# Recurrence input groups in a row, with the convolution read from the projection's PSUM banks

## The chip, the cores and the metric

One core of a Trainium2 chip runs one launch of a whole hybrid encoder layer. The metric is the device time in microseconds (us), the median over repeated runs. Names of engines: PE is TensorE, ACT is ScalarE, DVE is VectorE, POOL is GpSimd, SP is the queue that fetches the weights.

## What is computed

The layer has a residual stream of 512 tokens by 2048 channels. It is normalised and multiplied by one wide matrix w_in; the columns of the product are split among several consumers:

```
z = rms_norm(x, attn_norm) @ w_in
q_lat, kv_lat, k_rope_raw, g_mla, u_lru, g_lru, m_mla, m_lru = split(z)
xc = causal_dwconv(u_lru, conv_w, conv_b)          # 4 taps along the tokens, per channel
r = sigmoid(xc (block-wise) @ w_rg + b_rg)         # 16 blocks of 128 x 128
i = sigmoid(xc (block-wise) @ w_ig + b_ig)
log_a = -8 r softplus(-lam);  a = exp(log_a);  mult = sqrt(-expm1(2 log_a))
h = scan over tokens of  h[t] = a[t] h[t-1] + mult[t] i[t] xc[t]
y_lru = (h * silu(g_lru)) @ w_o_lru
y_mla = (attention(q_lat, kv_lat, k_rope_raw) * silu(g_mla)) @ w_o_mla
x = x + (sigmoid(m_mla) y_mla + sigmoid(m_lru) y_lru) @ w_out
```

A per-layer embedding with its own gate and a final norm follow. All is float32; products are kept accurate by splitting both operands into a high and a low part and adding three products.

## The kernel before

**Chunks.** The products with plain weights are made of chunks. A chunk is 128 rows of a weight matrix by 512 columns. For each chunk ACT writes its high part (whi, line 445, here called a split), POOL subtracts to get its low part (wlo, line 420), and PE runs 12 matmuls of 128 x 512 (lines 1544 and 1546 to 1554: four output tiles of 128 channels, three products each). The ring of split chunks holds four (RING), so the split of chunk k+4 waits until PE has finished chunk k (line 444). The ACT program is a list written by hand: a loop over the 16 chunks of a group, in each step ("slot k") the split for chunk k+4 and then whatever else has been placed at that k. Slot k can't begin before PE has finished chunk k of the current group.

**Groups.** A group is 16 chunks (K = 2048) that accumulate into four PSUM banks, one set of the two sets (0: banks 0 to 3, 1: banks 4 to 7). A set is claimed by PE when the semaphore released[set] has reached a number that is counted out (tables U_LRU, U_M2, U_LAT, lines 102 to 112). The stage that matters here runs these groups, in this order (lines 1681 to 1697): U0, U1, M2, U2, U3, Q, KV. U0 to U3 are the four groups of 512 channels of u_lru, M2 is the group of the last quarter of the merge gate m_mla, Q and KV are the latents. The last quarter of m_lru comes behind them, as the group M3.

**The recurrence of group i.** It needs these steps, on four tiles of 128 channels:

- DVE copies the four banks into upad, which has three zero columns in front (line 1206), releases the set, and makes the convolution of each tile from upad into xc with one tensor_scalar (line 1213) and three scalar_tensor_tensor (line 1216). After the second tile it makes gwlo (line 1220), the low part of the gate weights, and after each two tiles it makes xclo (line 999) from xc and ACT's xchi (line 598, lru_x).
- PE makes the gate products: gates(i, pair), line 1657, 12 matmuls for two tiles, in the middle of the group that follows: pair 0 behind its chunk 5+d, pair 1 behind its chunk 8+d (line 1678). They write into the set that group i itself had used.
- ACT makes the sigmoids r and i of a pair (lru_sigmoids, line 600, at slot 6+d and 8+d), the tanh (line 614), the exp (line 619, slot 9+d), the square (line 624, slot 10+d) and the square root (line 630, slot 11+d). Changes between these functions load another table on ACT.
- DVE multiplies ii by xc (line 1228), forms the argument of the root (line 1231), and then for each of four tiles does a multiply by the root (line 1236), the scan (line 1237) and the multiply by the output gate gg (line 1240). Only after these 12 operations does DVE go on to the next group.

In before the pairs use d = 0 for group 0 (inside U1), d = 4 for group 1 (inside M2), d = 0 for group 2 (inside U3) and d = 4 for group 3 (inside Q). Group U2 has no gate products in it.

**The merge gate.** When M2 is complete, ACT applies a sigmoid to its four banks into stage, and stores that (merge_gate_out, line 716, called at line 730, between two groups' loops, so behind slot 15 of M2 and ahead of slot 0 of U2).

**The latents.** DVE copies the four banks of Q (line 1247), computes the rotary angles, sums the squares, and so on; PE makes the sum of squares and the rotary keys' products behind chunk 12 of KV (line 1698).

Of the kernel before, what the change touches and what calls it, by code (L numbers as in the profile page):

```python
# [23 lines left out]
F32 = mybir.dt.float32  # L24
F32R = mybir.dt.float32r
# [38 lines left out]
def trunk_layer(nc, x, p, positions, vectors, conv_w, w_in, w_q_b, w_kv_b, w_rg, w_ig, w_o_mla, w_o_lru,  # L64
# [26 lines left out]
    C_M2 = C_LRU + 2 * KD  # L91
    C_LAT = C_M2 + 3 * KD
    C_U = (C_LRU, C_LRU + KD, C_M2 + KD, C_M2 + 2 * KD)
# [10 lines left out]
    U_LRU = (17, 18, 21, 21)  # L104
    SET_U = (1, 0, 0, 1)
    U_M2 = 20
# [24 lines left out]
    with ExitStack() as ctx:  # L131
# [14 lines left out]
        with ExitStack() as place:  # L146
# [36 lines left out]
        _, gg, upad, _, xc, xchi, xclo, rr, ii, _, graw, gwhi, gwlo = lay(  # L183
            ("lru_r1", [P, R1], F32), ("gg", [P, 4, S], F32),
            ("upad", [P, 4, S + 3], F32), ("upad_pad", [P, P - 16], F32), ("xc", [P, 4, S], F32), ("xchi", [P, 4, S], F32R),
            ("xclo", [P, 4, S], F32R), ("rr", [P, 4, S], F32), ("ii", [P, 4, S], F32),
            ("lru_pad", [P, R2 - 4 * S - P - 24 * S], F32),
            ("graw", [P, KD, 2 * P], F32), ("gwhi", [P, 4, 2 * P], F32R), ("gwlo", [P, 4, 2 * P], F32R))
        _, _, _, _, _, asq = lay(
            ("sq_r1", [P, R1], F32), ("sq_gg", [P, 4, S], F32), ("sq_upad", [P, 4, S + 3], F32),  # L190
            ("sq_pad", [P, P - 16], F32), ("sq_xc", [P, 4, S], F32), ("asq", [P, 4, S], F32))
# [125 lines left out]
        def _(sp):  # L317
# [46 lines left out]
            two_groups(C_M2, 0, ((w_in, m2), (w_in, COL_U + 2 * W)))  # L364
            two_groups(C_M2 + 2 * KD, 0, ((w_in, COL_U + 3 * W), (w_in, COL_Q)))
# [67 lines left out]
        def _(act):  # L433
# [176 lines left out]
            def lru_tanh(i, pair):  # L610
                if i == 0 and pair == 0:
                    act.wait_ge(sp_ready, 1)
                for t in (2 * pair, 2 * pair + 1):
                    act.activation(upad[:, t, 3:], rr[:, t], ACT.Tanh, scale=sp8[:, 4 * i + t:4 * i + t + 1]).then_inc(tanh_ready, 1)
# [11 lines left out]
            def lru_root(i):  # L626
                for t in range(4):

                    act.wait_ge(var_ready, 4 * i + t + 1)
                    act.activation(upad[:, t, 3:], upad[:, t, 3:], ACT.Sqrt).then_inc(mult_ready, 1)  # L630
# [14 lines left out]
            def lru_work(i, k, d):  # L645

                if k == 2 + d:
                    lru_x(i, 0)
                if k == 3 + d:
                    lru_x(i, 1)  # L650
                if k == 5 + d:
                    lru_x(i, 2)
                if k == 6 + d:
                    lru_x(i, 3)
                    lru_sigmoids(i, 0)
                if k == 7 + d:
# [67 lines left out]
            for k in range(KD):  # L724
                split(C_M2 + RING + k)
                if k == 3:
                    lru_out(0)
                lru_work(1, k, 4)
            act.wait_ge(z_stored, 16 * UNITS)
            merge_gate_out(0, 1, U_M2, sig_stored)  # L730
            for k in range(KD):
                split(C_U[2] + RING + k)
                if k == 8:
                    lru_out(1)
                if k == 10:
                    gate_weights(2)
            for k in range(KD):
                split(C_U[3] + RING + k)
                lru_work(2, k, 0)
                if k == 14:  # L740
                    gate_weights(3)
            for k in range(KD):
                split(C_LAT + RING + k)
                if k == 3:
                    lru_out(2)
                lru_work(3, k, 4)
                if k == 13:
                    act.dma_start(krw[:], w_in[:, COL_KR:COL_KR + QK_ROPE].rearrange("(k q) n -> q k n", q=P)).then_inc(krw_landed, 16)
                    act.dma_start(posi[:], positions.partition_broadcast(P)).then_inc(pos_landed, 16)
            for k in range(KD):  # L750
                split(C_LAT + RING + KD + k)
                if k == 6:
# [3 lines left out]
                if k == 8:  # L756
                    lru_out(3)
                    squares(latq, 0)
                if k == 10:
# [5 lines left out]
                if k == 13:  # L765
                    act.wait_ge(stage_stored, 16 * (2 * NG + 2))
                    latent_hi(latq, qlhi, 0)
                if k == 14:

                    act.wait_ge(kr_done, 1)  # L770
                    step(act.activation(krz[:], ps[:, 1], ACT.Copy))
                    act.sem_inc(released[0], 1)

                    for e in range(2):
                        act.dma_start(tsw[head_rows(1 - e)], krz[head_rows(e)]).then_inc(halves_swapped, 16)

            for n in range(KD + 2 * KL):
                c = C_M3 + n
                split(c + RING)
                if n == 0:  # L780
                    act.wait_ge(kr_summed, 1)
                    swap_quadrants(tmp[:, 4], tsw, 0)
# [208 lines left out]
        def _(dve):  # L991
# [209 lines left out]
            step(dve.memset(upad[:, :, 0:3], 0.0))  # L1201
            for i in range(NG):
                s = SET_U[i]
                dve.wait_ge(chunk_used, C_U[i] + KD)
                for m in range(4):
                    step(dve.tensor_copy(upad[:, m, 3:], ps[:, 4 * s + m]), wait=m == 3)
                signal(released[s])
                for m in range(4):

                    def tap(n):  # L1210
                        return vec[:, V_CW + n * KD + 4 * i + m:V_CW + n * KD + 4 * i + m + 1]

                    step(dve.tensor_scalar(xc[:, m], upad[:, m, 0:S], tap(0), vec[:, V_CB + 4 * i + m:V_CB + 4 * i + m + 1],
                                           ALU.mult, ALU.add))
# [12 lines left out]
                for t in range(4):  # L1227
                    step(dve.tensor_tensor(ii[:, t], ii[:, t], xc[:, t], ALU.mult), wait=t == 3)
                for t in range(4):
                    dve.wait_ge(decay_ready, 4 * i + t + 1)  # L1230
                    dve.scalar_tensor_tensor(upad[:, t, 3:], asq[:, t], 1.0, upad[:, t, 3:], ALU.add,
                                             ALU.mult).then_inc(var_ready, 1)
                for t in range(4):

                    dve.wait_ge(mult_ready, 4 * i + t + 1)
                    step(dve.tensor_tensor(ii[:, t], ii[:, t], upad[:, t, 3:], ALU.mult))
# [305 lines left out]
        def _(pe):  # L1542
# [153 lines left out]
            for k in range(KD):  # L1696
                chunk(C_LAT + KD + k, features, 1, hhi[:, k], hlo[:, k], k, KD)
                if k == 12:
# [266 lines left out]
```

## Time and profile before

| what | us |
|---|---|
| median of 3 runs | 1988.18 |
| lowest and highest of the 3 | 1986.60, 1988.99 |
| the profiled execution, device time | 1989.17 |
| its span, first to last instruction | 1987.4 |
| PE busy with matmuls | 1953.0 |
| DVE busy | 1083.2 |
| ACT busy | 785.4 |
| POOL busy | 620.6 |

The mean granted TensorE clock of the profiled execution is 0.995 of full speed. A busy time is the time in which the engine had an instruction running. Times in rows are counted from the start of the span. The stage described above lies between 618 and 964 us of it.

### The profile page before, as it was taken

What the parts mean: (1) busy time and instruction counts of PE and PEld (TensorE: products, weight loads), DVE (VectorE), ACT (ScalarE), POOL (GpSimd) and SP (SyncE); (2) the same over time, 40 slices, a digit from 0 to 9 for tenths busy, and PEclk for the clock granted to TensorE, in tenths of its full rate; (3) what the DMA queues carried; (4) which work ended last, traced back from release to release, by engine and by line L of the source; (5) the groups of instructions that cost most, each with busy time, mean ns of one, the idle gap of its engine ahead of it and who ended that gap; (6) DMA issues with size and microseconds to landing.
All of it is one profiled execution on the core that took longest, in us unless ns stands there. A gap on an engine that the chain in (4) does not pass through costs nothing.

```text
span 1987.4 us, 27817 instructions
## 1 busy us (share of the span) xinstructions
PE 1953.0 (98%) x10798; PEld 1708.9 (86%) x10798; DVE 1083.2 (55%) x1571; ACT 785.4 (40%) x1259; POOL 620.6 (31%) x463
## 2 busy tenths in 40 slices
PE   7999999999999999999999999999999999999996
PEld 6889999999998887887788888888888888888885
DVE  4867778788883584587856557661011330111444
ACT  6434444444443446446345545422222222333323
POOL 3000000000003454454452223254444454444452
PEclk9999999999999999999999999999999999999998
DMA  6444444444445333334352334253333443225232
GB/s 245 129 137 127 135 132 126 134 126 137 128 128 172 105 116 123 131 106 143 94 150 86 127 106 149 81 216 107 126 116 127 137 170 104 88 87 210 86 105 106
DMA packets 210727, 256.26 MB, mean 129 GB/s; under 512 B 20749, under 2 KB 144309, under 8 KB 203061
## 3 DMA queue, kind: packets, MB, share of 16 engines
q1 hardware_dynamic: 195792, 185.11, 30.4%
q10 hardware_dynamic: 14821, 69.56, 9.3%
q8 instruction: 80, 1.31, 0.3%
q14 instruction: 34, 0.28, 0.0%
HBM read 218.45 MB, written 33.55 MB: 127 GB/s over the span
## 4 chain that ended last, share of the span: by engine, by line
issue 70%; POOL 26%; PE 1%; DVE 1%; POOLq 1%; ACT 1%; DMA 0%; ACTq 0%; DVEq 0%
POOL wlo L420 26%; PE ps L1544 1%; POOLq L419 1%; DMA ropec<-in_rope_const 0%; ACT hhi L486 0%; POOLq L429 0%; DVE x L1533 0%; DVE hlo L1055 0%; DVE sqj L1037 0%; ACT xraw L467 0%; DVE x L1506 0%; DVE stage L1505 0%; DVE x L1536 0%; ACT whi L445 0%; POOL wlo L427 0%
## 5 line engine op out<-in xcount | busy, mean ns | idle before, releaser
L420 POOL TENSOR_TENSOR wlo<-raw,whi 128x512 fp32r<-128x512 f32 x448 | 614.2, 1375 | 1328.8 <-ACT whi L445 1327.8
L445 ACT ACTIVATE whi<-raw 128x512 fp32r<-128x512 f32 x480 | 299.7, 631 | 777.7 <-PE ps L1544 727.9
L1544 PE MATMUL ps<-hhi,whi 128*128 128x512 f32 x640 | 250.0, 391 | 2.1 <-POOL wlo L420 2.1
L1544 PE MATMUL ps<-hlo,whi 128*128 128x512 f32 x640 | 249.1, 389 | 0.0
L1544 PE MATMUL ps<-hhi,wlo 128*128 128x512 f32 x640 | 249.0, 389 | 0.0
L1651 PE MATMUL ps<-shi,cut 128*128 128x256 f32 x768 | 217.3, 283 | 0.0
L1652 PE MATMUL ps<-slo,cut 128*128 128x256 f32 x768 | 217.3, 283 | 0.0
L1653 PE MATMUL ps<-shi,cut 128*128 128x256 f32 x768 | 217.3, 283 | 0.0
L573 ACT ACTIVATE cut<-wblock 128x768 fp32r<-128x768 f32 x96 | 81.1, 845 | 270.8 <-PE ps L1653 270.3
L1652 PE MATMUL ps<-hlo,cut 128*128 128x256 f32 x576 | 163.0, 283 | 0.0
L1653 PE MATMUL ps<-hhi,cut 128*128 128x256 f32 x576 | 163.0, 283 | 0.0
L1651 PE MATMUL ps<-hhi,cut 128*128 128x256 f32 x576 | 163.0, 283 | 0.0
L1651 PEld LDWEIGHTS ps<-shi,cut 128*128 128x128 f32 x768 | 147.5, 192 | 0.0
L1652 PEld LDWEIGHTS ps<-slo,cut 128*128 128x128 f32 x768 | 147.5, 192 | 0.0
L1653 PEld LDWEIGHTS ps<-shi,cut 128*128 128x128 f32 x768 | 147.5, 192 | 0.0
L1544 PEld LDWEIGHTS ps<-hhi,whi 128*128 128x128 f32 x640 | 120.4, 188 | 28.3 <-POOL wlo L420 2.2
L1544 PEld LDWEIGHTS ps<-hhi,wlo 128*128 128x128 f32 x640 | 120.2, 188 | 25.1
L1544 PEld LDWEIGHTS ps<-hlo,whi 128*128 128x128 f32 x640 | 120.3, 188 | 25.0 <-issue 0.2
L999 DVE TENSOR_TENSOR cut<-tw,cut 128x1024 fp32r<-128x1024 f32 x96 | 117.0, 1219 | 0.0
L1651 PEld LDWEIGHTS ps<-hhi,cut 128*128 128x128 f32 x576 | 110.6, 192 | 0.0
L1652 PEld LDWEIGHTS ps<-hlo,cut 128*128 128x128 f32 x576 | 110.6, 192 | 0.0
L1653 PEld LDWEIGHTS ps<-hhi,cut 128*128 128x128 f32 x576 | 110.6, 192 | 0.0
(284 smaller groups left out, 4141.1 us busy)
## 6 DMA issues: line engine op xcount, KB each, us to landing
wblock<-in_w_in SPq DMA_DIRECT2D x384, 128.0 KB, 2.5
raw<-in_w_in SPq DMA_DIRECT2D x40, 1024.0 KB, 5.0
raw<-in_w_o_lru SPq DMA_DIRECT2D x16, 1024.0 KB, 5.0
raw<-in_w_o_mla SPq DMA_DIRECT2D x16, 1024.0 KB, 5.0
raw<-in_w_out SPq DMA_DIRECT2D x16, 1024.0 KB, 5.0
raw<-in_w_ple_gate SPq DMA_DIRECT2D x16, 1024.0 KB, 5.0
gate_scr<-stage ACTq DMA_DIRECT2D x16, 512.0 KB, 3.5
raw<-in_w_kv_b SPq DMA_DIRECT2D x32, 256.0 KB, 4.0
```

Of the source, the lines that this page charges most:

```text
L419: pool.wait_ge(hi_ready, i * (2 * RAWC) + (c0 + k + 1))
L420: pool.tensor_tensor(wlo[:, k % RING], raw[:, k // RAWC, k % RAWC], whi[:, k % RING].bitcast(F32), ALU.subtract).then_inc(lo_ready, 1)
L445: act.activation(whi[:, c % RING], raw[:, c // RAWC % 2, c % RAWC], ACT.Copy).then_inc(hi_ready, 1)
L573: act.activation(cut[:, 0, W11:T1], quarters(n)[:, 0:3], ACT.Copy).then_inc(cut_whi, 1)
L999: return dve.tensor_tensor(out_, whole, hi.bitcast(F32), ALU.subtract)
L1544: return pe.matmul(o, l, r, start=start, stop=stop)
L1651: pe.matmul(o, h, ahi, start=k == 0 and i % 2 == 0, stop=False, skip_group_check=True)
L1652: pe.matmul(o, h, alo, start=False, stop=False, skip_group_check=True)
L1653: ins = pe.matmul(o, l, ahi, start=False, stop=last, skip_group_check=True)
```

## The change

The four input groups U0 to U3 follow each other, M2 comes behind them, then Q and KV. The sets are now 1, 0, 1, 0 for U0 to U3 and 1 for M2. The convolution reads the PSUM banks itself: the first operation multiplies by the tap of the current token and adds the bias over the whole row, the other three add the earlier tokens into xc from column 1, 2 and 3 on, so no zero columns and no copy are needed. The set is released when the convolution of all four tiles is done. gwlo is made ahead of the convolution, and the four xclo behind it. The two sigmoid pairs are awaited separately. On ACT xchi comes at slots 1+d, 2+d, 3+d and 3+d, the first sigmoids at slot 5+d, the rest as before; the root goes to slot 0 of the next group where d is 4 or more. The offsets d are 0 for group 0 (inside U1), 2 for group 1 (inside U2), 4 for group 2 (inside U3) and 5 for group 3 (inside M2). The merge gate's sigmoids come at slot 1 of Q. In KV several latent steps come three slots or so sooner.

```diff
-    C_U = (C_LRU, C_LRU + KD, C_M2 + KD, C_M2 + 2 * KD)
+    C_U = tuple(C_LRU + n * KD for n in range(NG))
-    U_LRU = (17, 18, 21, 21)
-    SET_U = (1, 0, 0, 1)
-    U_M2 = 20
+    U_LRU = (17, 18, 20, 21)
+    SET_U = (1, 0, 1, 0)
+    U_M2 = 23
...
-            two_groups(C_M2, 0, ((w_in, m2), (w_in, COL_U + 2 * W)))
-            two_groups(C_M2 + 2 * KD, 0, ((w_in, COL_U + 3 * W), (w_in, COL_Q)))
+            two_groups(C_LRU + 2 * KD, 0, ((w_in, COL_U + 2 * W), (w_in, COL_U + 3 * W)))
+            two_groups(C_M2, 0, ((w_in, m2), (w_in, COL_Q)))
...
             def lru_work(i, k, d):
-                if k == 2 + d:
-                    lru_x(i, 0)
-                if k == 3 + d:
-                    lru_x(i, 1)
-                if k == 5 + d:
-                    lru_x(i, 2)
-                if k == 6 + d:
-                    lru_x(i, 3)
-                    lru_sigmoids(i, 0)
-                if k == 7 + d:
+                if k in (1 + d, 2 + d):
+                    lru_x(i, k - 1 - d)
+                if k == 3 + d:
+                    lru_x(i, 2)
+                    lru_x(i, 3)
+                if k == 5 + d:
+                    lru_sigmoids(i, 0)
+                if k == 6 + d:
                     lru_tanh(i, 0)
                     lru_gate_in(i)
...
-                if k == 11 + d:
+                if k == 11 + d and d < 4:
                     lru_root(i)
...
             for k in range(KD):
-                split(C_M2 + RING + k)
+                split(C_U[2] + RING + k)
                 if k == 3:
                     lru_out(0)
-                lru_work(1, k, 4)
-            act.wait_ge(z_stored, 16 * UNITS)
-            merge_gate_out(0, 1, U_M2, sig_stored)
-            for k in range(KD):
-                split(C_U[2] + RING + k)
-                if k == 8:
-                    lru_out(1)
-                if k == 10:
-                    gate_weights(2)
+                lru_work(1, k, 2)
             for k in range(KD):
                 split(C_U[3] + RING + k)
-                lru_work(2, k, 0)
-                if k == 14:
+                if k == 1:
+                    gate_weights(2)
+                if k == 5:
+                    lru_out(1)
+                lru_work(2, k, 4)
+            for k in range(KD):
+                split(C_M2 + RING + k)
+                if k == 0:
+                    lru_root(2)
+                if k == 2:
                     gate_weights(3)
+                if k == 6:
+                    lru_out(2)
+                lru_work(3, k, 5)
             for k in range(KD):
                 split(C_LAT + RING + k)
-                if k == 3:
-                    lru_out(2)
-                lru_work(3, k, 4)
+                if k == 0:
+                    lru_root(3)
+                if k == 1:
+                    act.wait_ge(z_stored, 16 * UNITS)
+                    merge_gate_out(0, 1, U_M2, sig_stored)
+                if k == 7:
+                    lru_out(3)
...
             for i in range(NG):
                 s = SET_U[i]
+                dve.wait_ge(gw_hi, i + 1)
+                step(dve.tensor_tensor(gwlo[:], graw[:, 4 * i:4 * i + 4], gwhi[:].bitcast(F32), ALU.subtract))
+                signal(gw_lo)
                 dve.wait_ge(chunk_used, C_U[i] + KD)
                 for m in range(4):
-                    step(dve.tensor_copy(upad[:, m, 3:], ps[:, 4 * s + m]), wait=m == 3)
-                signal(released[s])
-                for m in range(4):
...
-                    step(dve.tensor_scalar(xc[:, m], upad[:, m, 0:S], tap(0), vec[:, V_CB + 4 * i + m:V_CB + 4 * i + m + 1],
-                                           ALU.mult, ALU.add))
-                    for n in range(1, 4):
-                        step(dve.scalar_tensor_tensor(xc[:, m], upad[:, m, n:n + S], tap(n), xc[:, m], ALU.mult, ALU.add))
+                    u = ps[:, 4 * s + m]
+                    step(dve.tensor_scalar(xc[:, m], u, tap(3), vec[:, V_CB + 4 * i + m:V_CB + 4 * i + m + 1], ALU.mult, ALU.add))
+                    for late in range(1, 4):
+                        step(dve.scalar_tensor_tensor(xc[:, m, late:], u[:, 0:S - late], tap(3 - late), xc[:, m, late:], ALU.mult, ALU.add))
                     signal(xc_ready)
-                    if m == 1:
-                        dve.wait_ge(gw_hi, i + 1)
-                        step(dve.tensor_tensor(gwlo[:], graw[:, 4 * i:4 * i + 4], gwhi[:].bitcast(F32), ALU.subtract))
-                        signal(gw_lo)
-                    if m % 2:
-                        for t in (m - 1, m):
-                            dve.wait_ge(xc_hi, 4 * i + t + 1)
-                            lo_of(xclo[:, t], xc[:, t], xchi[:, t]).then_inc(xc_lo, 1)
-                dve.wait_ge(ri_ready, 8 * i + 8)
+                signal(released[s])
                 for t in range(4):
+                    dve.wait_ge(xc_hi, 4 * i + t + 1)
+                    lo_of(xclo[:, t], xc[:, t], xchi[:, t]).then_inc(xc_lo, 1)
+                for t in range(4):
+                    if t % 2 == 0:
+                        dve.wait_ge(ri_ready, 8 * i + 2 * t + 4)
                     step(dve.tensor_tensor(ii[:, t], ii[:, t], xc[:, t], ALU.mult), wait=t == 3)
...
             whole_group(C_U[0], SET_U[0], U_LRU[0])
             whole_group(C_U[1], SET_U[1], U_LRU[1], 0, 0)
-            whole_group(C_M2, 1, U_M2, 1, 4)
-            whole_group(C_U[2], SET_U[2], U_LRU[2])
-            whole_group(C_U[3], SET_U[3], U_LRU[3], 2, 0)
-            whole_group(C_LAT, 0, U_LAT[0], 3, 4)
+            whole_group(C_U[2], SET_U[2], U_LRU[2], 1, 2)
+            whole_group(C_U[3], SET_U[3], U_LRU[3], 2, 4)
+            whole_group(C_M2, 1, U_M2, 3, 5)
+            whole_group(C_LAT, 0, U_LAT[0])
...
-                if k == 12:
+                if k == 9:
                     claim(0, U_LAT[0] + 1)
                     square_sum(0, 1)
```

## Rows read from the trace of the kernel before

**Rows 1.** The page, busy time, share of the span and instructions of each engine.
```profile
PE 1953.0 (98%) x10798; PEld 1708.9 (86%) x10798; DVE 1083.2 (55%) x1571; ACT 785.4 (40%) x1259; POOL 620.6 (31%) x463
```

**Rows 2.** Waits of PE: who waited for whom, total us, times, longest us.
```profile
PE ps L1544 <- ACTq L608: 3.6, 2, 1.8
PE ps L1544 <- POOL wlo L420: 2.1, 2, 1.7
...
PE ps L1544 <- DVE krw L999: 0.3, 1, 0.3
```

**Rows 3.** Timeline of PE: start us, us, instruction, [idle before it, who ended it].
```profile
678.46 0.39 PE L1544 MATMUL ps<-xchi,gwhi 128*128 128x512 f32 x1
...
689.11 0.39 PE L1544 MATMUL ps<-hhi,wlo 128*128 128x512 f32 x1
689.61 0.50 PE L1544 MATMUL ps<-xchi,gwhi 128*128 128x512 f32 x1
...
751.58 0.50 PE L1544 MATMUL ps<-xchi,gwhi 128*128 128x512 f32 x1 [1.83 <-ACTq L608]
...
756.48 0.39 PE L1544 MATMUL ps<-hhi,wlo 128*128 128x512 f32 x1
...
776.98 0.50 PE L1544 MATMUL ps<-hhi,whi 128*128 128x512 f32 x1 [1.73 <-POOL wlo L420]
...
898.76 0.50 PE L1544 MATMUL ps<-xchi,gwhi 128*128 128x512 f32 x1 [1.80 <-ACTq L608]
...
903.23 0.40 PE L1544 MATMUL ps<-hhi,whi 128*128 128x512 f32 x1
```

**Rows 4.** Stretches: busy us (instructions) of PE, PEld, DVE, ACT, POOL, then PEclk, DMA share, GB/s.
```profile
752.00:756.00 4.00, 4.00 (x13) 3.15 (x12) 0.00 (x0) 3.15 (x7) 2.57 (x2) 0.62 0.77 267
...
899.00:903.00 4.00, 4.00 (x12) 3.08 (x12) 0.00 (x0) 3.31 (x6) 2.57 (x2) 0.59 0.71 244
```

**Rows 5.** Timeline of ACT, group 0: its last sigmoid, its roots.
```profile
693.63 0.69 ACT L606 ACTIVATE ii<-ps,vec 128x512 f32<-128x512 f32 x1
...
704.62 2.19 ACT L630 ACTIVATE upad<-upad 128x512 f32<-128x512 f32 x4
```

**Rows 6.** Timeline of DVE: last part of group 0, start of group 1; last part of group 2.
```profile
701.34 4.19 DVE L1231 SCALAR_TENSOR_TENSOR upad<-asq,upad 128x512 f32<-128x512 f32 x4 [4.49 <-ACT asq L624]
705.46 0.68 DVE L1236 TENSOR_TENSOR ii<-ii,upad 128x512 f32<-128x512 f32 x1
...
721.36 1.59 DVE L1240 TENSOR_TENSOR gg<-gg,xc 128x512 f32<-128x512 f32 x1
723.10 2.48 DVE L1206 COPY upad<-ps 128x512 f32<-128x512 f32 x4
...
852.38 0.68 DVE L1236 TENSOR_TENSOR ii<-ii,upad 128x512 f32<-128x512 f32 x1
...
868.24 1.59 DVE L1240 TENSOR_TENSOR gg<-gg,xc 128x512 f32<-128x512 f32 x1
```

**Rows 7.** Forms of DVE's operations: duration ns min/median/max, first and last start us.
```profile
L1216 DVE SCALAR_TENSOR_TENSOR xc<-upad,vec,xc x48: 750/752/1872, 665.6 to 892.5; 128x512 f32<-128x512 f32 x48
L1476 DVE SCALAR_TENSOR_TENSOR x1lo<-ps,vec,x1hi x16: 750/751/753, 1698.0 to 1831.1; 128x512 fp32r<-128x512 f32 x16
L1283 DVE TENSOR_SCALAR tmp<-ps x2: 691/692/692, 950.7 to 984.2; 128x512 f32<-128x512 f32 x2
L1220 DVE TENSOR_TENSOR gwlo<-graw,gwhi x4: 1224/1659/2327, 673.7 to 881.4; 128x1024 fp32r<-128x1024 f32 x4
L999 DVE TENSOR_TENSOR xclo<-xc,xchi x16: 677/693/1779, 675.1 to 895.0; 128x512 fp32r<-128x512 f32 x16
L1237 DVE TENSOR_TENSOR_SCAN xc<-rr,ii x16: 1224/1225/2197, 706.2 to 930.5; 128x512 f32<-128x512 f32 x16
L1240 DVE TENSOR_TENSOR gg<-gg,xc x16: 692/1601/1830, 707.4 to 931.8; 128x512 f32<-128x512 f32 x16
```

**Rows 8.** Timeline of ACT: the merge gate's sigmoids between the loops of two groups.
```profile
771.42 2.07 ACT L719 ACTIVATE stage<-ps 128x512 f32<-128x512 f32 x4
```

More of the change, by code:

```diff
@@ L90, in trunk_layer @@
     C_LRU = C_M + 2 * KD
-    C_M2 = C_LRU + 2 * KD
-    C_LAT = C_M2 + 3 * KD
-    C_U = (C_LRU, C_LRU + KD, C_M2 + KD, C_M2 + 2 * KD)
+    C_U = tuple(C_LRU + n * KD for n in range(NG))
+    C_M2 = C_LRU + NG * KD
+    C_LAT = C_M2 + KD
     C_M3 = C_LAT + 2 * KD
@@ L182, in trunk_layer @@
         _, swhole, _ = lay(("seven_r12", [P, R1 + R2], F32), ("swhole", [P, 4, KD // 2, H], F32), ("whole_pad", [P, 8], F32))
-        _, gg, upad, _, xc, xchi, xclo, rr, ii, _, graw, gwhi, gwlo = lay(
+        _, gg, mult, xc, xchi, xclo, rr, ii, _, graw, gwhi, gwlo = lay(
             ("lru_r1", [P, R1], F32), ("gg", [P, 4, S], F32),
-            ("upad", [P, 4, S + 3], F32), ("upad_pad", [P, P - 16], F32), ("xc", [P, 4, S], F32), ("xchi", [P, 4, S], F32R),
+            ("mult", [P, 4, S], F32), ("xc", [P, 4, S], F32), ("xchi", [P, 4, S], F32R),
             ("xclo", [P, 4, S], F32R), ("rr", [P, 4, S], F32), ("ii", [P, 4, S], F32),
-            ("lru_pad", [P, R2 - 4 * S - P - 24 * S], F32),
+            ("lru_pad", [P, R2 - 28 * S], F32),
             ("graw", [P, KD, 2 * P], F32), ("gwhi", [P, 4, 2 * P], F32R), ("gwlo", [P, 4, 2 * P], F32R))
-        _, _, _, _, _, asq = lay(
-            ("sq_r1", [P, R1], F32), ("sq_gg", [P, 4, S], F32), ("sq_upad", [P, 4, S + 3], F32),
-            ("sq_pad", [P, P - 16], F32), ("sq_xc", [P, 4, S], F32), ("asq", [P, 4, S], F32))
+        _, _, _, _, asq = lay(
+            ("sq_r1", [P, R1], F32), ("sq_gg", [P, 4, S], F32), ("sq_mult", [P, 4, S], F32),
+            ("sq_xc", [P, 4, S], F32), ("asq", [P, 4, S], F32))
         (_, qlhi, qllo, kvhi, kvlo, cosT, sinT, latq, latkv, tsw, krz, tmp, krw, krw2, posi, _, krhi, krlo0, krlo1) = lay(
@@ L613, in lru_tanh @@
                 for t in (2 * pair, 2 * pair + 1):
-                    act.activation(upad[:, t, 3:], rr[:, t], ACT.Tanh, scale=sp8[:, 4 * i + t:4 * i + t + 1]).then_inc(tanh_ready, 1)
+                    act.activation(mult[:, t], rr[:, t], ACT.Tanh, scale=sp8[:, 4 * i + t:4 * i + t + 1]).then_inc(tanh_ready, 1)
             def lru_decay(i):
@@ L629, in lru_root @@
                     act.wait_ge(var_ready, 4 * i + t + 1)
-                    act.activation(upad[:, t, 3:], upad[:, t, 3:], ACT.Sqrt).then_inc(mult_ready, 1)
+                    act.activation(mult[:, t], mult[:, t], ACT.Sqrt).then_inc(mult_ready, 1)
             def lru_gate_in(i):
@@ L751, in _ @@
                 split(C_LAT + RING + KD + k)
-                if k == 6:
+                if k == 5:
                     act.wait_ge(krw_landed, 16)
                     act.activation(krw2[:, :, 0:QK_ROPE], krw[:], ACT.Copy).then_inc(krw_hi, 1)
-                if k == 8:
-                    lru_out(3)
+                if k == 4:
                     squares(latq, 0)
-                if k == 10:
+                if k == 6:
                     act.wait_ge(angle_ready, 1)
@@ L762, in _ @@
                     act.activation(tmp[:, 2], tmp[:, 0], ACT.Sin, scale=0.5).then_inc(sin_ready, 1)
-                if k == 12:
+                if k == 9:
                     root(TT + 1)
-                if k == 13:
+                if k == 10:
                     act.wait_ge(stage_stored, 16 * (2 * NG + 2))
                     latent_hi(latq, qlhi, 0)
-                if k == 14:
+                if k == 12:
                     act.wait_ge(kr_done, 1)
@@ L775, in _ @@
                         act.dma_start(tsw[head_rows(1 - e)], krz[head_rows(e)]).then_inc(halves_swapped, 16)
+                if k == 14:
+                    act.wait_ge(kr_summed, 1)
+                    swap_quadrants(tmp[:, 4], tsw, 0)
             for n in range(KD + 2 * KL):
@@ L779, in _ @@
                 split(c + RING)
-                if n == 0:
-                    act.wait_ge(kr_summed, 1)
-                    swap_quadrants(tmp[:, 4], tsw, 0)
                 if n == 1:
@@ L1199, in _ @@
             signal(sp_ready)
-            step(dve.memset(upad[:, :, 0:3], 0.0))
             for i in range(NG):
                 s = SET_U[i]
+                dve.wait_ge(gw_hi, i + 1)
+                step(dve.tensor_tensor(gwlo[:], graw[:, 4 * i:4 * i + 4], gwhi[:].bitcast(F32), ALU.subtract))
+                signal(gw_lo)
                 dve.wait_ge(chunk_used, C_U[i] + KD)
-                for m in range(4):
-                    step(dve.tensor_copy(upad[:, m, 3:], ps[:, 4 * s + m]), wait=m == 3)
-                signal(released[s])
                 for m in range(4):
@@ L1230, in _ @@
                     dve.wait_ge(decay_ready, 4 * i + t + 1)
-                    dve.scalar_tensor_tensor(upad[:, t, 3:], asq[:, t], 1.0, upad[:, t, 3:], ALU.add,
+                    dve.scalar_tensor_tensor(mult[:, t], asq[:, t], 1.0, mult[:, t], ALU.add,
                                              ALU.mult).then_inc(var_ready, 1)
@@ L1235, in _ @@
                     dve.wait_ge(mult_ready, 4 * i + t + 1)
-                    step(dve.tensor_tensor(ii[:, t], ii[:, t], upad[:, t, 3:], ALU.mult))
+                    step(dve.tensor_tensor(ii[:, t], ii[:, t], mult[:, t], ALU.mult))
                     step(dve.tensor_tensor_scan(xc[:, t], rr[:, t], ii[:, t], 0.0, ALU.mult, ALU.add))
@@ L1697, in _ @@
                 chunk(C_LAT + KD + k, features, 1, hhi[:, k], hlo[:, k], k, KD)
-                if k == 12:
+                if k == 9:
                     claim(0, U_LAT[0] + 1)
```

2 lines of the change are left out of this document (1 added, 1 removed).

## The prediction

> **What bounds the kernel now.** I read the busy shares first: PE is busy for 1953.0 of 1987.4 us [rows 1], so time can only be won where PE stands still or runs slowly, and is lost wherever a new order makes it do so. Next the waits of PE [rows 2]: in the stage that the change touches it waits 3.6 us for ACT, 2.1 us for POOL and 0.3 us for krw. The timeline of PE gives the places [rows 3]. Matmuls start 0.2267 us apart (47 of them from 678.46 to 689.11), so a chunk or a pair of gate products (12 matmuls) takes 2.72 us. The waits are: 0.27 us ahead of the second pair of group 0 (689.61), 1.83 us ahead of the second pair of group 1 (751.58), 1.73 us in U2 (776.98), 1.80 us ahead of the second pair of group 3 (898.76). The gap's idle time starts at the modelled end of a matmul, 0.39 us behind its start, so each of the three long gaps costs 0.16 us more. Behind two of them the clock is low [rows 4]: 0.62 and 0.59 of full speed in four microseconds, so close to the lower level of 1.2 GHz. The 14 starts from 751.58 to 756.48 take 4.90 us in place of 3.17, and the 12 from 898.76 to 903.23 take 4.47 in place of 2.72: 1.7 us each. Behind 776.98 no such loss is seen.
>
> **What the change wins.** Before, ACT reaches the first sigmoids only after the last xchi, and PE waits for it to free the set. Now the sigmoids of pair 0 stand one slot sooner and nothing of xchi stands near them, so they end about 2 us behind the pair's products (four starts 0.6 us apart, the last of 0.69 [rows 5]) while pair 1 comes 8.16 us behind those. The gaps of groups 0, 1 and 3 go: 0.3, 1.83 + 0.16 + 1.7 and 1.80 + 0.16 + 1.7, 7.6 us. The merge gate's sigmoids (2.07 us [rows 8], behind a table load) no longer follow the roots with no split between them: now slot 1 of Q splits first, the splits behind the sigmoids are then about 4.4 us late, and PE needs that chunk 8.16 us behind the slot's beginning, of which split and wlo take 2. This wins 1.9 us. The krw wait and a small step at the end of KV, 0.5 us, go as the latents' copy no longer stands in DVE's queue behind the recurrence. Sum: 10.0 us won. The fetches keep their number and size and only change order; SP has them in flight a row of chunks ahead, so I put them at nothing.
>
> **What the convolution costs on DVE.** A tile was one tensor_scalar and three scalar_tensor_tensor from upad, of 0.75 us where undisturbed, up to 1.87 us [rows 7], behind four copies (2.48 us [rows 6]). With a PSUM source the nearest rows are 0.69 us for a tensor_scalar and 0.751 us for a scalar_tensor_tensor, and the latter lies between 750 and 753 ns in all 16 cases, next to POOL's running wlo too [rows 7]. So a tile costs 0.69 + 3 x 0.75 + 0.12 (three steps between) + 0.15 (signal) = 3.2 us, four of them 12.8 us. Bounds: 11 us if the shortened rows gained, 15 us if they could be held up as those from upad.
> The Trainium skill, page "VectorE: DVE Perf Modes", section on the TRN2 errata, gives 120 cycles plus one per element at 0.96 GHz for a PSUM source, thus 0.66 us for every one of the 16. By it the four tiles would take 1.2 us less; the rows above decide, and the page's rule would only shorten each stall below by 1.2 us (3.7 us in all).
>
> **What the new order asks of DVE.** This is the step that decides. Let G be the start of a group's second pair of gate products on PE, and E the end of its last multiply on DVE. Before, for group 0, G = 689.61 [rows 3]; the last sigmoid ends at 694.32 and the first root starts at 704.62 [rows 5]; DVE's 12 closing operations run from 705.46 to 722.95, 17.5 us [rows 6], and E - G = 33.3 us. In group 2 the same 12 take 17.45 us (852.38 to 869.83 [rows 6]). Undisturbed they would take 4 x (0.68 + 1.22 + 0.69) + 0.5 = 10.9 us; the scan's median is near its minimum, but its maximum is 2.20, and the multiply by gg has a median of 1.60 against a minimum of 0.69 [rows 7]: operations with both inputs in SBUF are held up by POOL's wlo, one of which comes every 2.72 us. The change leaves these 12 as they are, and POOL's rhythm too. The second sigmoids end about 0.5 us sooner behind G, so E - G = 32.9 us.
> From E to the first xclo of the next group DVE now needs: 0.15 + gwlo 1.66 (median, 1.22 to 2.33 [rows 7]) + 0.15 + the convolution 12.8 + release 0.15 + xclo 0.69 [rows 7] + 0.1 to PE = 15.7 us. Before, xclo came behind two tiles, not four, but copy and hold-ups made that as long, and PE asked for it later.
> PE's own way from G of group i to pair 0 of group i+1 is: 1 pair, and (7 - d) chunks of the group, and (6 + d') of the next, that is 14 + d' - d units of 2.72 us. For groups 0 to 1 (d 0, d' 2) and 1 to 2 (2, 4) it is 16 units, 43.5 us; for 2 to 3 (4, 5) 15 units, 40.8 us. Before, it was 18 units for 0 to 1, and a whole group more for 1 to 2.
> **Stalls.** 32.9 + 15.7 = 48.6 us against 43.5: PE waits 5.1 us ahead of pair 0 of group 1, and again 5.1 us at group 2. Check by the clock: G(0) = 689.34 now, E(0) = 722.2, first xclo seen at 737.9; U2 starts at 711.1 and its chunk 7 ends at 732.9; wait 5.0. For group 3, the root of group 2 stands one slot later (slot 0 of M2, not 11+4), so its roots start at G + 16.3 and the 12 operations at 16.5 in place of 15.4: E - G = 34.0, and 34.0 + 15.7 - 40.8 = 8.9 us. Sum 19.0 us. Queued behind: ACT stands at xchi for the late xc (its slot 6 of U2 begins at 737.5, 7.4 us late), but PE itself is waiting for the same tiles then, and the three chunks behind the pair are split in time (slot 6's wlo is there at 739.6, needed at 746). I put that at nothing; its cover is PE's own stall.
> **Clock.** Each of the three stalls is longer than the gaps behind which 1.7 us were lost [rows 3, 4]; none, as behind 776.98, to twice 1.7 us each are possible. I take 1.7: 5.1 us.
> **Sum**: 19.0 + 5.1 - 10.0 = +14.1 us. On the profiled execution (span 1987.4, 1989.2 with what lies around it, 1.0 above the median of 1988.2) this is 2003.3; on the median 2002.3.
>
> **Rivals.**
> (1) DVE's closing operations aren't held up, or much less, in the new order (E - G of about 26). Then groups 1 and 2 are in time by 2 us, group 3 is late by 27.1 + 15.7 - 40.8 = 2.0 us, and nearly all of the 10.0 stays: 1980. It decides from E - G below 27.8 us. Against it: two chains in the rows with 17.5 us, and POOL's work doesn't change. For it: only that hold-ups hang on phase.
> (2) Half of it: E - G near 30, stalls of 2.2, 2.2 and 6.0 without a low clock, 10.4 against 10.0 won: 1988.6, no change.
> (3) Worse than forecast: the convolution is held up too (15 us in place of 12.8), and each stall brings 2.3 us of low clock: 19.0 + 6.6 + 6.9 - 10.0 = +22.5, 2011.
> (4) The gains don't come, since the merge gate's sigmoids and the late latents wait elsewhere; with the stalls that gives 2006 to 2008.
>
> **How the numbers follow.** About 0.2% (4 us) can be told from no change here. My forecast with cases (3) and (4) has 0.80, of which (3) and (4) hold 0.15; case (1) 0.13; case (2) and what lies around it 0.07. The likeliest, 2002.3, is the prediction. Its own range is 1995 to 2008: each stall by 1.5 us either way, the clock from none to 2.3 each. To leave out no more than 2 in 10 it reaches down to case (2) and up towards (3): 1988 to 2010. Faster 0.13, within 0.2% 0.07, slower 0.80.
>
> **What would show it.** In the waits of PE: three waits of 5, 5 and 9 us at gate products (pair 0 of groups 1, 2, 3), released by xclo or by the DVE release of the set; none released by ACT's line of sigmoids, none by wlo at the merge gate. In the timeline of DVE: convolution operations of 0.69 and 0.75 us that are never longer, and 17 us for the 12 closing operations. The clock low behind each stall. Wrong would be: closing operations in 11 us, or no wait of PE at pair 0 of group 1.

## The result, and the profile after

The changed kernel takes 2001.28 us (median of 6 runs, 2000.95 to 2002.83), the kernel before 1987.74 us in the same comparison (6 runs). The ratio is 1.007 with a 95% interval of 1.0057 to 1.0083: slower by 13.5 us. The profiled execution took 2001.37 us, with a span of 1999.6.

The waits of PE in the changed kernel (who waited for whom, total us, times, longest us), which answer to [rows 2]:
```profile
PE ps L1544 <- DVE xclo L1003: 17.6, 3, 7.6
...
PE ps L1544 <- POOL wlo L420: 0.2, 1, 0.2
```
All that PE waited for in this stage before (ACT's line 608, wlo behind the merge gate, krw) is gone, and one new cause stands in its place: DVE's xclo, three times. The 0.2 us for wlo lies outside the stage.

The timeline of PE at these three places (start us, us, instruction, [idle before it, who ended it]), which answers to [rows 3]:
```profile
731.51 0.39 PE L1544 MATMUL ps<-hhi,wlo 128*128 128x512 f32 x1
736.78 0.77 PE L1544 MATMUL ps<-xchi,gwhi 128*128 128x512 f32 x1 [4.88 <-DVE xclo L1003]
...
740.75 0.39 PE L1544 MATMUL ps<-xchi,gwhi 128*128 128x512 f32 x1
...
749.63 0.39 PE L1544 MATMUL ps<-xchi,gwhi 128*128 128x512 f32 x1
...
798.44 0.77 PE L1544 MATMUL ps<-xchi,gwhi 128*128 128x512 f32 x1 [5.12 <-DVE xclo L1003]
...
859.72 0.77 PE L1544 MATMUL ps<-xchi,gwhi 128*128 128x512 f32 x1 [7.59 <-DVE xclo L1003]
```
Each wait stands at the first matmul of pair 0, of groups 1, 2 and 3. From here on, G is the start of a group's second pair of gate products on PE and E the end of its last multiply on DVE, as in the prediction; 749.63 is G of group 1. The nine intervals from 736.78 to 740.75 take 3.97 us where 2.04 would do (nine times 0.2267): 1.9 us of low clock. The stretches behind the waits (columns as in [rows 4]) show it at exactly half, 1.2 GHz:
```profile
736.00:740.00 4.00, 3.22 (x8) 2.58 (x9) 4.00 (x4) 3.02 (x5) 2.99 (x2) 0.50 0.01 2
798.00:802.00 4.00, 3.56 (x9) 2.82 (x10) 4.00 (x4) 3.02 (x6) 3.05 (x2) 0.50 0.00 0
859.00:863.00 4.00, 3.28 (x8) 2.63 (x9) 4.00 (x4) 3.02 (x5) 3.04 (x2) 0.50 0.00 0
```

The timeline of DVE from group 0 to group 1, and the end of group 2, which answers to [rows 6]:
```profile
699.52 4.19 DVE L1231 SCALAR_TENSOR_TENSOR mult<-asq,mult 128x512 f32<-128x512 f32 x4 [5.79 <-ACT asq L624]
703.63 0.68 DVE L1236 TENSOR_TENSOR ii<-ii,mult 128x512 f32<-128x512 f32 x1
...
719.46 1.60 DVE L1240 TENSOR_TENSOR gg<-gg,xc 128x512 f32<-128x512 f32 x1
721.21 1.23 DVE L1208 TENSOR_TENSOR gwlo<-graw,gwhi 128x1024 fp32r<-128x1024 f32 x1
722.58 0.81 DVE L1217 TENSOR_SCALAR xc<-ps,vec 128x512 f32<-128x512 f32 x1
...
735.94 4.67 DVE L1003 TENSOR_TENSOR xclo<-xc,xchi 128x512 fp32r<-128x512 f32 x4 [0.25 <-DVE xc L1219]
...
827.64 0.73 DVE L1236 TENSOR_TENSOR ii<-ii,mult 128x512 f32<-128x512 f32 x1 [0.97 <-ACT mult L630]
...
842.41 1.60 DVE L1240 TENSOR_TENSOR gg<-gg,xc 128x512 f32<-128x512 f32 x1
```
The closing operations run from 703.63 to 721.06, 17.4 us, and DVE goes from them to gwlo, convolution and xclo with no idle time but 0.15 to 0.25 us between steps: when PE wants the first xclo at 731.7, DVE is in the third of four tiles.

The forms of the convolution and of the closing operations (duration ns min/median/max, first and last start), which answer to [rows 7]:
```profile
L1219 DVE SCALAR_TENSOR_TENSOR xc<-ps,vec,xc x48: 746/749/751, 662.6 to 857.9; 128x511 f32<-128x511 f32 x16, 128x510 f32<-128x510 f32 x16, 128x509 f32<-128x509 f32 x16
L1217 DVE TENSOR_SCALAR xc<-ps,vec x16: 810/810/812, 661.7 to 855.5; 128x512 f32<-128x512 f32 x16
...
L1237 DVE TENSOR_TENSOR_SCAN xc<-rr,ii x16: 1224/1225/2335, 704.3 to 900.6; 128x512 f32<-128x512 f32 x16
L1240 DVE TENSOR_TENSOR gg<-gg,xc x16: 691/1602/1828, 705.6 to 902.8; 128x512 f32<-128x512 f32 x16
```
From the banks none of the 64 operations is ever held up (48 within 5 ns); the closing operations still are. The merge gate's sigmoids (start 891.17 in ACT's timeline) no longer make PE wait.

### The profile page after: what moved, and what is told of

It is laid out like the page before. It is cut to its first block, busy times and chain, and to the rows that moved or that the text cites. A ratio compares the mean times of both kernels' runs of the same rounds, so it can differ in the third digit from the quotient of the medians.

```text
span 1999.6 us, 27800 instructions
## 1 busy us (share of the span) xinstructions
PE 1953.5 (98%) x10798; PEld 1710.2 (86%) x10798; DVE 1062.4 (53%) x1554; ACT 786.8 (39%) x1260; POOL 615.1 (31%) x463
## 4 chain that ended last, share of the span: by engine, by line
issue 71%; POOL 25%; PE 1%; DVE 1%; POOLq 1%; ACT 1%; DMA 0%; ACTq 0%; DVEq 0%
POOL wlo L420 25%; PE ps L1544 1%; POOLq L419 1%; DMA ropec<-in_rope_const 0%; ACT hhi L486 0%; POOLq L429 0%; DVE x L1533 0%; DVE hlo L1059 0%; DVE sqj L1041 0%; ACT xraw L467 0%; DVE x L1506 0%; DVE stage L1505 0%; DVE x L1536 0%; ACT whi L445 0%; POOL wlo L427 0%
```

## The experiments

The theory under test is that of the prediction: the convolution, ACT's slots and the later place of the merge gate's sigmoids win about 10 us, and the closed-up order loses more, because DVE's chain from one group to the next is longer than PE's way there. Each ratio below is to the kernel before, run beside it (medians 1988.45, 1988.38 and 1987.44 us).

**The good parts without the order.** conv_merge is the kernel before with its old order and offsets, the new convolution, the new slots, and the merge gate's sigmoids behind a split:
```diff
 (buffers, convolution block, xchi and sigmoid slots as in the change; the root at 11 + d as before; and:)
-            act.wait_ge(z_stored, 16 * UNITS)
-            merge_gate_out(0, 1, U_M2, sig_stored)
             for k in range(KD):
                 split(C_U[2] + RING + k)
+                if k == 1:
+                    act.wait_ge(z_stored, 16 * UNITS)
+                    merge_gate_out(0, 1, U_M2, sig_stored)
```


> The kernel before with its old order of groups (U0, U1, M2, U2, U3, Q, KV) and offsets (0, 4, 0, 4), but with the convolution read from the banks, the xchi and sigmoid slots of the change, and the merge gate's sigmoids at slot 1 of U2. My theory (the convolution and the slots win, only the closed-up order loses): DVE has two or four chunks more from one group to the next, so no wait of PE at pair 0; the waits at the second pairs of groups 0, 1 and 3 (7.6 us) and at the merge gate (1.9 us) go: 1978, PE waits in the stage under 1 us. Rival (the convolution from the banks is itself what costs, since it holds the set until the end): slower than before, 1990 or more, with PE waiting for xclo. Second rival (the waits of before are set by something else): 1986 to 1988.

Measured: 1978.45 us (5 runs), ratio to before 0.9954 (0.994 to 0.9967). The waits of PE that are left (the 0.2 us for wlo lies outside the stage):
```profile
PE ps L1539 <- DVE krw L998: 0.2, 1, 0.2
PE ps L1539 <- POOL wlo L420: 0.2, 1, 0.2
```
The rival, that the convolution from the banks is what costs, falls for the old order. This kernel beats both. No run parts the convolution from ACT's new slots, so how the gain divides between these two is not shown.

conv_only is the same, with merge_gate_out left between the two loops.

> The same without moving the merge gate's sigmoids. Theory: 1980, the one wait of 1.7 us for wlo behind the merge gate stays and the others go. Rival (convolution costs): 1990 or more.

Measured: 1981.31 us, ratio 0.9966 (0.9954 to 0.9978), 1.3 us above the expectation, and PE waits 1.7 us for wlo behind the merge gate, as before (the longest of the three in this line):
```profile
PE ps L1538 <- POOL wlo L420: 2.2, 3, 1.7
```

merge_only is the kernel before with the merge gate's lines alone moved, as in the last diff.

> The kernel before with one edit: the merge gate's sigmoids at slot 1 of U2 in place of between the two loops. Theory: only the wait for wlo at 777 us goes, 1.9 us, thus 1985.8. Rival (the late splits are caused by the roots alone): no change, 1987.7.

Measured: 1985.32 us, ratio 0.9986 (0.9977 to 0.9995), some 3 us won where 1.9 was expected. The wait for wlo at 777 us is gone. The rest fits a low clock that failed to come in the profiled execution (1.7 us; the krw wait grew from 0.3 to 0.7): behind the wait of 1.8 us at the second pair of group 3 the granted clock stays full here, while behind that of group 1 it is low again.
```profile
751.00:755.00 4.00, 3.92 (x12) 3.11 (x13) 0.00 (x0) 3.52 (x6) 2.57 (x2) 0.68 0.66 227
...
896.00:900.00 4.00, 3.77 (x16) 3.11 (x17) 0.00 (x0) 3.88 (x8) 2.60 (x2) 1.00 0.60 205
```

**The order alone.** order_only has the changed order, sets, offsets and merge gate, with the buffers, lru_work and the convolution block of before (and the root at the changed place).

> The changed order of groups, offsets (0, 2, 4, 5) and merge gate, but the convolution from upad and the xchi and sigmoid slots of before. Theory: the first xclo comes as late behind the closing operations as with the new convolution (about 15 us), so PE waits 5, 5 and 8 us at pair 0 of groups 1, 2, 3; and on top the second pairs wait for the sigmoids behind the fourth xchi, some 3.5 us and 1.7 us of low clock in each of three groups: 2015 to 2022. Rival (the order costs nothing, the convolution from the banks does): 1988 to 1990.

Measured: 1996.85 us (4 runs), ratio 1.0046 (1.0031 to 1.0061). Slower than before, as the theory has it, so the order by itself costs. But the time lies 18 us below the lower end that I gave, and the sizes are a miss: the waits at pair 0 are shorter than in the changed kernel, and the second pairs hardly wait.
```profile
PE ps L1550 <- DVE xclo L1005: 11.9, 3, 5.1
...
PE ps L1550 <- ACTq L608: 0.6, 1, 0.6
```
The low clock was also less in the profiled execution, the fastest of the four (1994.57 us): behind the first of two waits of 3.4 us the granted clock was 1.00 (736 to 740 us), behind the second 0.57 (795 to 799 us).

The timelines (DVE's, and one line of PE's) say why the first xclo is sooner:
```profile
720.17 1.60 DVE L1246 TENSOR_TENSOR gg<-gg,xc 128x512 f32<-128x512 f32 x1
721.91 2.48 DVE L1212 COPY upad<-ps 128x512 f32<-128x512 f32 x4
...
732.48 1.22 DVE L1226 TENSOR_TENSOR gwlo<-graw,gwhi 128x1024 fp32r<-128x1024 f32 x1
733.85 3.30 DVE L1005 TENSOR_TENSOR xclo<-xc,xchi 128x512 fp32r<-128x512 f32 x2
737.08 0.54 DVE L1219 TENSOR_SCALAR xc<-upad,vec 128x512 f32<-128x512 f32 x1
...
735.61 0.47 PE L1550 MATMUL ps<-xchi,gwhi 128*128 128x512 f32 x1 [3.37 <-DVE xclo L1005]
```
With the set free after the copies, two tiles are enough for pair 0: PE starts it at 735.61, 13.9 us behind E (721.77), against 15.7 us in the changed kernel. I had also expected the second pairs to wait 3.5 us each for the sigmoids; only one waits, 0.6 us. My reading is that the stall at pair 0 moves pair 1 back by the same amount and DVE works on through it; no run tests that alone. So in this order the new convolution block makes the first xclo later, not sooner: the two parts of the change work against each other. With the merge gate moved in all four kernels, the new block and slots bring the old order from 1985.32 (merge_only) to 1978.45, and the new order from 1996.85 to 2001.28: they win 7 us in the one and lose 4 in the other.

**Is it the first xclo, or the set?** xclo_sooner puts the first two xclo behind tile 1 in the changed kernel:
```diff
                     signal(xc_ready)
-                signal(released[s])
-                for t in range(4):
-                    dve.wait_ge(xc_hi, 4 * i + t + 1)
-                    lo_of(xclo[:, t], xc[:, t], xchi[:, t]).then_inc(xc_lo, 1)
+                    if m == 3:
+                        signal(released[s])
+                    if m % 2:
+                        for t in (m - 1, m):
+                            dve.wait_ge(xc_hi, 4 * i + t + 1)
+                            lo_of(xclo[:, t], xc[:, t], xchi[:, t]).then_inc(xc_lo, 1)
```


> The changed kernel with the xclo of tiles 0 and 1 made right behind the convolution of tile 1, as before the change, and the set still released behind tile 3. Theory A (pair 0 writes into all four banks, so behind the first xclo the release of the set is the next bound, and it comes later by the two xclo): each wait grows by 1 to 2 us: 2004 to 2007. Rival B (only the first xclo holds PE up): it comes 6 us sooner, groups 1 and 2 no longer wait: 1984 to 1988.

Measured: 2005.64 us, ratio 1.0091 (1.0074 to 1.0108). The waits before pair 0 are 1.07, 5.61, 5.50 and 7.98 us; the last is put down to DVE's queue, the others to nothing that the profile shows ("issue"), and none to xclo:
```profile
679.88 0.47 PE L1546 MATMUL ps<-xchi,gwhi 128*128 128x512 f32 x1 [1.07 <-issue]
...
740.18 0.76 PE L1546 MATMUL ps<-xchi,gwhi 128*128 128x512 f32 x1 [5.61 <-issue]
...
863.17 0.77 PE L1546 MATMUL ps<-xchi,gwhi 128*128 128x512 f32 x1 [7.98 <-DVEq L1000]
```
The timeline of DVE at group 1 gives the release:
```profile
731.88 1.30 DVE L1003 TENSOR_TENSOR xclo<-xc,xchi 128x512 fp32r<-128x512 f32 x2
...
737.25 2.32 DVE L1219 SCALAR_TENSOR_TENSOR xc<-ps,vec,xc 128x511 f32<-128x511 f32 x3
740.17 1.29 DVE L1003 TENSOR_TENSOR xclo<-xc,xchi 128x512 fp32r<-128x512 f32 x2 [0.60 <-DVE xc L1219]
```
The first two xclo are done at 733.18, yet PE starts at 740.18, 7 us later, with DVE's first operation behind the fourth tile; at group 3 the two start at 863.17 and 863.16. Theory A holds: reading the banks directly ties them up until the fourth tile, and pair 0 writes to all four. The three waits grew by only 0.7, 0.4 and 0.4 us where 1 to 2 was expected, and group 0 has a new one of 1.07. The copy into upad, 2.6 us of DVE with its wait, had bought an early release: in order_only the copies end 2.6 us behind E, in the changed kernel the fourth tile ends 14.6 us behind it.

**What stretches the closing operations.** short_wlo takes the work of POOL's wlo away, as far as it can; the kernel leaves out the low parts of the other 480 columns, and every wait and signal stays (the loop behind the stage, as before, isn't shown):
```diff
-            with pool.Fori(0, (C_END - C_LRU) // (2 * RAWC)) as i:
+            with pool.Fori(0, 2) as i:
+                low_parts(C_LRU, i)
+            with pool.Fori(0, (C_M3 - C_LRU - KD) // (2 * RAWC)) as i:
+                short_parts(C_LRU + KD, i)
...
```


> The changed kernel, with one thing taken away: from U1 to KV, POOL's subtraction for wlo covers 32 of the 512 columns (the low parts of those weights are left out for the other columns; every wait and signal stays). Theory (DVE's operations with both inputs in SBUF are held up by POOL's wlo): the 12 closing operations of a group take 11 us in place of 17.2, the waits of PE at pair 0 of groups 1 and 2 vanish and that of group 3 falls from 7.6 to under 2 us, the low clock goes too: 1979 to 1981. Rival (the closing operations are long by themselves, or by ACT and DMA): 17 us and 2001, as before.

> The same edit in the kernel before, as a control (the same low parts left out). Theory: the closing operations shrink to 11 us here too, but nothing waits for them; only the waits for ACT at the second pairs of groups 1 and 3 may shrink, since the convolution from upad isn't held up either: 1980 to 1986. If it gained as much as the changed kernel does from the same edit (20 us), wlo itself would be the bound: 1967.

Measured: the changed kernel with it takes 1979.96 us (ratio 0.996, 0.9945 to 0.9976), the kernel before with it 1978.36 us (0.9952, 0.9937 to 0.9968). The edit is worth 21 us in the changed kernel and 10 in the kernel before, and the two come to within 2 us of each other. In the changed kernel with short wlo, the closing operations of group 0:
```profile
703.39 0.69 DVE L1248 TENSOR_TENSOR ii<-ii,mult 128x512 f32<-128x512 f32 x1 [1.45 <-ACT mult L642]
...
713.31 0.69 DVE L1252 TENSOR_TENSOR gg<-gg,xc 128x512 f32<-128x512 f32 x1
714.15 1.23 DVE L1220 TENSOR_TENSOR gwlo<-graw,gwhi 128x1024 fp32r<-128x1024 f32 x1
```
They take 10.6 us in place of 17.4, and PE waits for xclo once, 1.7 us, at group 3, where its own way is 40.8 us long and not 43.5. The control came out 1.6 us below the lower end I had given: its waits at the second pairs vanish altogether, since with nothing holding DVE up the fourth xc is ready in time.

The trace of before had shown the same without any edit, in group 1, which the prediction left out when it took its 17.5 us from groups 0 and 2. There the roots and the merge gate's sigmoids follow each other on ACT with no split between, so POOL has no wlo to make from 768.28 to 774.68:
```profile
768.75 0.68 DVE L1236 TENSOR_TENSOR ii<-ii,upad 128x512 f32<-128x512 f32 x1
...
781.44 1.60 DVE L1240 TENSOR_TENSOR gg<-gg,xc 128x512 f32<-128x512 f32 x1
...
774.68 10.76 POOL L420 TENSOR_TENSOR wlo<-raw,whi 128x512 fp32r<-128x512 f32 x6 [6.40 <-ACT whi L445]
```
The closing operations took 14.3 us there, and those that ran before 774.68 took their shortest times.

The Trainium skill, page "SBUF — State Buffer", section "SBUF: two separate sides", has a rule for this: GpSimd and VectorE share a pair of SBUF ports, and a VectorE operation with two SBUF inputs and a GpSimd one that reads SBUF exclude each other for the whole instruction. These runs agree with it: with two SBUF inputs the median multiply by gg is 1.60 us and falls to 0.69 with short wlo, and with one input in PSUM all 48 stay at 0.75. The exclusion goes both ways: a wlo takes 1.29 us by itself, and one that started at 713.66 in the changed kernel, while DVE's chain ran, took 2.25.

**Moving one slot.** later_one raises the offset of group 1:
```diff
-                lru_work(1, k, 2)
+                lru_work(1, k, 4)
...
-                if k == 11 + d and d < 4:
+                if k == 11 + d and (d < 4 or i == 1):
...
-            whole_group(C_U[2], SET_U[2], U_LRU[2], 1, 2)
+            whole_group(C_U[2], SET_U[2], U_LRU[2], 1, 4)
```


> The changed kernel with the offset of group 1 raised from 2 to 4 (its root at slot 15). Theory (from G of a group to pair 0 of the next DVE needs 48 us, so what one transition gains the next loses): the wait at group 1 goes (from 4.9 to 0), that at group 2 grows from 5.1 to 10.5, group 3 stays at 7.6; one low clock less: 2000, within 2 us of the changed kernel. Rival (each wait is a slot chosen too early by itself): 1994.5.

Measured: 1999.41 us, ratio 1.0056 (1.0042 to 1.0069), against 1.007 for the changed kernel.
```profile
796.48 0.76 PE L1544 MATMUL ps<-xchi,gwhi 128*128 128x512 f32 x1 [9.47 <-DVE xclo L1003]
...
857.82 0.77 PE L1544 MATMUL ps<-xchi,gwhi 128*128 128x512 f32 x1 [7.59 <-DVE xclo L1003]
```
The wait at group 1 is gone, that at group 2 is 9.5 (10.5 expected), that at group 3 is 7.59 as before. The waits of a stretch of groups are a sum (17.6 us before this edit, 17.1 with it) that the offsets in its middle move about and don't remove; what is won is mainly one low clock. The offset of the last group is another matter: by the prediction's count of units, 14 + d' - d for each transition, the sum hangs on the first and the last offset alone. An estimate from that: raising group 3's from 5 to 7, two chunks of 2.72 us, would take 5.4 us off its wait. No run tried it.

**A longer chain on DVE.** extra_copies puts four copies ahead of each convolution:
```diff
                 for m in range(4):
+                    step(dve.tensor_copy(xc[:, m], ps[:, 4 * s + m]))
+                for m in range(4):
```


> The changed kernel with four more copies (each bank into xc, overwritten by the convolution) ahead of each group's convolution: 2.9 us more of DVE per group. Theory (DVE is the bound between groups): each of the three waits grows by 2.9 us, and pair 0 of group 0 begins to wait about 1.2 us: 2001.3 + 8.7 + 1.2 = 2011. Rival (PE waits for ACT or a set that another frees): less than 3 us more.

Measured: 2013.46 us, ratio 1.0128 (1.0111 to 1.0145). The waits are 1.33, 7.77, 7.77 and 10.48 us: 2.9, 2.7 and 2.9 more than 4.88, 5.12 and 7.59. Whatever DVE is given here, PE pays. The time is 2.5 us above the expected 2011: the low clock behind the later waits lasted longer (1.9, 2.2 and 2.4 us in place of 1.8 to 1.9), and the profiled execution came to the first gate product 1.6 us later than that of the changed kernel, its new wait there not counted, which the edit doesn't explain.

**The root one slot sooner.** root_sooner drops the condition on d and the call at slot 0 of M2:
```diff
-                if k == 11 + d and d < 4:
+                if k == 11 + d:
...
-                if k == 0:
-                    lru_root(2)
```


> The changed kernel with the root of group 2 in slot 15 of U3 in place of slot 0 of M2. Theory: DVE's idle 0.97 us ahead of the closing operations of group 2 goes, and the wait at pair 0 of group 3 falls by as much, to 6.6: 2000.3. Rival (ACT's late place costs nothing): 2001.3.

Measured: 2001.80 us, ratio 1.0072 (1.0058 to 1.0086), no gain. The theory's detail fails. The idle 0.97 us goes (the closing operations of group 2 start at 826.87), but the wait at group 3 stays at 7.6:
```profile
826.87 0.68 DVE L1234 TENSOR_TENSOR ii<-ii,mult 128x512 f32<-128x512 f32 x1
...
828.84 1.83 DVE L1238 TENSOR_TENSOR gg<-gg,xc 128x512 f32<-128x512 f32 x1
830.59 1.78 DVE L1234 TENSOR_TENSOR ii<-ii,mult 128x512 f32<-128x512 f32 x1
...
860.03 0.77 PE L1542 MATMUL ps<-xchi,gwhi 128*128 128x512 f32 x1 [7.62 <-DVE xclo L1001]
```
In the changed kernel the same two operations are these:
```profile
829.66 0.69 DVE L1240 TENSOR_TENSOR gg<-gg,xc 128x512 f32<-128x512 f32 x1
830.27 1.78 DVE L1236 TENSOR_TENSOR ii<-ii,mult 128x512 f32<-128x512 f32 x1
```
This execution runs 0.3 us later as a whole (G of group 2 at 811.45 and not 811.17), so the chain began 1.1 us sooner. The first multiply by gg then fell together with a wlo (828.84) and took 1.83 us in place of 0.69, which gives the 1.1 us back: from the next operation on, both chains stand at the same times, 0.3 us apart.

## Why the prediction was right

It gave 2002.3 us; measured was 2001.28, and the range (1988 to 2010) and the direction hold. So does the mechanism: three waits at pair 0 of groups 1, 2 and 3, released by xclo, and DVE's chain as their cause. That the total came within 1 us is in part luck: the stalls came out 0.9 us shorter than forecast and the low clock 0.6 us longer.

- **DVE's way (right, to a tenth).** From G to E it said 32.9 us. Measured: group 0 32.85 (688.21 to 721.06), group 1 33.1 (749.63 to 782.72), group 2 32.8 (811.17 to 844.01). From E to PE's first gate product it said 15.7: 736.78 - 721.06 = 15.7, and 15.7 again at groups 2 and 3. The parts under it were off both ways and cancelled: a tensor_scalar from PSUM took 0.81 us and not 0.69, so a tile 3.3 and not 3.2, and gwlo 1.23 and not 1.66. At group 1 gwlo started at 721.21, ahead of a wlo at 721.76, and it was the wlo that took longer (1.82 us).
- **Stalls.** Said 5.1, 5.1, 8.9 (19.0); measured start to start 5.04, 5.28, 7.75 (18.1). The term that was mis-sized is that of group 3: the root's later slot, put at 1.1 us, cost nothing. The closing operations did begin as late as forecast (16.5 us behind G), but took 16.4 us in place of 17.5, so E - G was 32.8 and not 34.0; root_sooner showed it from the other side.
- **Clock.** Said 1.7 us each, 5.1; measured 1.9, 1.8 and 1.9, together 5.7. It was low behind all three.
- **What was won.** Said 10.0. The waits named are all gone. With 18.1 + 5.7 = 23.8 us lost, the medians (13.5 us apart) leave 10.3 won, and the two profiled executions (12.2 us apart) 11.6. Of these 11.6, 1.1 lie ahead of the first gate product, which comes at 677.33 and not 678.46 (so G of group 0 is 688.21, where the prediction's check had 689.34); the prediction named no gain in front of it, and other kernels' executions come there between 677.18 (conv_merge) and 678.05 (later_one), so this much is put down to the execution and not to the change. conv_merge, where nothing is lost, won 9 to 10 us.
- **Costs put at nothing.** SP's changed order of fetches, and ACT's late splits: PE has no wait for wlo in the stage and none for a fetch in the changed kernel, so the late splits were covered and the fetches cost nothing that shows.
- **The rivals.** (1) needed closing operations of 11 us; short_wlo is that case made by hand, and gave 1980.0, the figure of the rival. (2) needed E - G near 30, and it was 32.8 to 33.1. (3) fell with the forms of the convolution, and (4) with the waits, of which none is at the merge gate or the latents.
- **The table of costs.** The Trainium skill, page "VectorE: DVE Perf Modes", section on the TRN2 errata, gives 120 cycles plus one per element at 0.96 GHz for a PSUM source, an estimate of 0.66 us for each operation. They took 0.75 and 0.81 us, so the measurement decides.
- **What the prediction missed** is that the new block made the first xclo later in this order. It said "copy and hold-ups made that as long"; order_only shows 13.9 us for the old block against 15.7 for the new. In before, the first xclo of group 1 starts 14.0 us behind E (736.93 against 722.95), in order_only 12.1 (733.85 against 721.77). The hold-ups shrink there: ACT stands at xchi for the late xc (3.64 us ahead of 728.46, 2.82 ahead of 732.43), its splits stop meanwhile and POOL's wlo with them (at 724.89, 729.69 and 733.65, where before has one every 2.7 us), and the first tile takes 3.8 us in place of 4.8. It doesn't change the forecast, which used the new block's length.

## What to carry to other kernels

When stages with a serial chain on another engine are moved closer together, compare that chain's full length from one stage to the next (with its hold-ups as the trace shows them, not the minimum durations) with the bounding engine's way between the same two points; shifting the slots in the middle of the stretch only moves the difference about. Reading PSUM directly saves a copy, but it ties the banks up to the last reader, so look who claims them next. The parts of a change are worth running apart, and in both combinations: here the new block and slots won 7 us in the old order and lost 4 in the new one, and the order, with the latents' sooner steps, cost 12 us with the old block and 23 with the new.

## What was not expected of the hardware

- A start of a DVE chain that came 1.1 us sooner (826.87 in place of 827.64, in an execution 0.3 us later) brought its end no gain: one of its operations met a wlo and took 1.83 us in place of 0.69.
- Behind waits of PE of 1.8 us the granted clock was low in some places (0.62 at 752 us before) and full in others (1.00 at 896 us in merge_only); behind two waits of 3.4 us in one execution of order_only it was 1.00 and 0.57; behind the changed kernel's waits of 4.9 to 7.6 us it was low, 0.50, each time. So two executions of one kernel can differ by some 1.7 us, which fits the runs of before: 5 of the 16 run beside conv_merge took 1986.8 to 1987.2 us at a mean granted clock of 0.996 or 0.997, the other 11 took 1988.2 to 1989.6 at 0.995.
- A tensor_scalar that reads PSUM took 0.81 us with two per-partition scalars (16 of them, 810 to 812 ns), and 0.69 us with two constants [rows 7].
